# Split operands for the value products and memory scores of a hybrid decoder layer, with other warm-up products and other places for the turns of x

## Time and profile before

| | us |
|---|---|
| median of 3 runs | 573.56 (573.34 to 574.38) |
| profiled execution | 572.92 |
| its span, first to last instruction | 571.1 |
| TensorE busy | 562.1 (98%) |
| VectorE busy | 425.9 (75%) |
| ScalarE busy | 406.6 (71%) |

### The profile page before, as it was taken

How to read it: one execution, slowest core, us unless ns; L and a number is a source line. 1 busy time by engine, 2 the same in 40 slices (tenths; PEclk the granted TensorE clock), 3 DMA queues, 4 the chain that set the end, 5 groups by cost and what they waited for, 6 DMA issues and landing times.

```text
span 571.1 us, 8602 instructions
## 1 busy us (share of the span) xinstructions
PE 562.1 (98%) x2640; PEld 468.0 (82%) x2640; DVE 425.9 (75%) x716; ACT 406.6 (71%) x651; POOL 2.1 (0%) x26
## 2 busy tenths in 40 slices
PE   8999999999999999999999999999999999999994
PEld 7888888888888888888888888888888888888884
DVE  4769769678886877866756768668568886877975
ACT  5786866967868778776784784875598786855543
POOL 1000000000000000000000000000000000000000
PEclk9999999999999999999999999999999999999998
DMA  8997769568676776886875976779799986983803
GB/s 272 353 280 238 210 173 250 169 201 230 190 233 192 200 216 188 234 224 163 250 215 157 264 199 192 220 194 299 246 229 266 260 248 187 260 230 111 244 2 147
DMA packets 151236, 123.32 MB, mean 216 GB/s; under 512 B 66809, under 2 KB 133162, under 8 KB 150698
## 3 DMA queue, kind: packets, MB, share of 16 engines
q1 hardware_dynamic: 151112, 122.98, 76.3%
q10 hardware_dynamic: 98, 0.03, 0.0%
HBM read 105.93 MB, written 2.10 MB: 189 GB/s over the span
## 4 chain that ended last, share of the span: by engine, by line
PE 98%; DVE 1%; ACT 0%; POOL 0%; issue 0%; ACTq 0%; POOLq 0%
PE ps L614 28%; PE ps L615 28%; PE ps L616 28%; PE ps L697 2%; PE ps L650 1%; PE ps L654 1%; PE ps L658 1%; PE ps L679 1%; PE ps L850 1%; PE ps L855 1%; PE ps L851 1%; PE ps L637 1%; PE ps L772 1%; PE ps L624 0%; PE ps L818 0%; PE ps L682 0%
## 5 line engine op out<-in xcount | busy, mean ns | idle before, releaser
L1209 DVE TENSOR_TENSOR w_lo<-w_raw,w_hi 128x1024 fp32r<-128x1024 f32 x183 | 222.5, 1222 | 106.2 <-ACT w_hi L880 104.2
L880 ACT ACTIVATE w_hi<-w_raw 128x1024 fp32r<-128x1024 f32 x183 | 192.6, 1057 | 82.3 <-PE ps L616 81.3
L614 PE MATMUL ps<-w_hi,aT 128*128 128x512 f32 x540 | 211.8, 392 | 0.0
L615 PE MATMUL ps<-w_lo,aT 128*128 128x512 f32 x540 | 210.3, 389 | 0.0
L616 PE MATMUL ps<-w_hi,aT 128*128 128x512 f32 x540 | 210.1, 389 | 0.0
L616 PEld LDWEIGHTS ps<-w_hi,aT 128*128 128x128 f32 x540 | 101.4, 188 | 21.2
L614 PEld LDWEIGHTS ps<-w_hi,aT 128*128 128x128 f32 x540 | 101.4, 188 | 21.0
L615 PEld LDWEIGHTS ps<-w_lo,aT 128*128 128x128 f32 x540 | 101.4, 188 | 20.4
L614 PE MATMUL ps<-w_hi,yT_hi 128*128 128x512 f32 x144 | 56.2, 390 | 0.0
L616 PE MATMUL ps<-w_hi,yT_lo 128*128 128x512 f32 x144 | 56.0, 389 | 0.0
L615 PE MATMUL ps<-w_lo,yT_hi 128*128 128x512 f32 x144 | 56.0, 389 | 0.0
(11 more groups left out here) (202 smaller groups left out, 569.1 us busy)
## 6 DMA issues: line engine op xcount, KB each, us to landing
w_raw<-in_w_in SPq DMA_DIRECT2D x251, 256.0 KB, 3.2
w_raw<-in_w_out SPq DMA_DIRECT2D x64, 256.0 KB, 4.0
w_raw<-in_w_kv_mem SPq DMA_DIRECT2D x32, 256.0 KB, 4.5
w_raw<-in_w_q_mem SPq DMA_DIRECT2D x16, 256.0 KB, 3.0
w_raw<-in_w_o_mem SPq DMA_DIRECT2D x16, 256.0 KB, 3.8
mems<-in_mem SPq DMA_DIRECT2D x1, 2048.0 KB, 10.1
xs<-in_x SPq DMA_DIRECT2D x3, 512.0 KB, 6.3
w_raw<-in_w_in SPq DMA_DIRECT2D x10, 128.0 KB, 5.5
```

What stands on the lines that cost most here:

```text
L614: pe.matmul(acc, hi[:, k0 + k, tok], w_hi[:, slot, k], start=first and k == 0, stop=False)
L615: pe.matmul(acc, hi[:, k0 + k, tok], w_lo[:, slot, k], start=False, stop=False)
L880: act.activation(w_hi[:, i % SPLITS], raw, ACT.Copy).then_inc(hi_made, 1)
L1209: dve.tensor_tensor(lo, w_raw[:, i % RAW], hi.bitcast(F32), ALU.subtract).then_inc(lo_made, 1)
```

## The change

- Value products: `v_sb` becomes `v_hi` (ScalarE, same instruction) and `v_lo` (VectorE, at n = 3 and 4); `probT` gets a high copy (ScalarE, behind the merge at n = 4) and a low difference (VectorE, n = 5). Each of the three products of a head becomes three fp32r products. VectorE's `silu_piece` stands at n = 4, 6, 7, 8. `probT_hi`, `probT_lo` and `v_lo` live in tiles that were free then.
- Memory scores: both banks of turned queries and the turned keys are split into high parts (ScalarE) and low parts (VectorE), and each of the 8 products becomes three fp32r products.
- Warm-up: 10 and 6 products instead of 3 and 2, of a 128x128 tile of ones that VectorE sets; TensorE waits for that tile and no longer for the identity in front of them.
- x turns: row blocks 2 and 3 inside k-tile 1, 4 and 5 inside k-tile 3, both ahead of the tile's last pair of products. The three gain vectors are loaded from SP's queue behind half 2 and turned behind k-tile 6.
- Lambda: the product that spreads it has 128 rows: the tile of ones, and a column that is zero except in its first element.

```diff
-ROWS_BEHIND = {0: (2,), 1: (3,), 2: (4, 5), 4: (6, 7), 6: (8, 9, 10, 11), 10: (12, 13, 14, 15)}
+ROWS_AMID = {1: (2, 3), 3: (4, 5)}
+ROWS_BEHIND = {4: (6, 7), 6: (8, 9, 10, 11), 10: (12, 13, 14, 15)}
-WARM_UP = (3, 2)
+WARM_UP = (10, 6)
+SILU_AT = (4, 6, 7, 8)
...
 # SP, load of the first halves
+                if n == 2:
+                    for row, vec in ((0, norm_mem_g), (KO, mem_norm_g)):
+                        sp.dma_start(gains[row:row + KO, :], ...).then_inc(gains_loaded, 16)
+                    sp.dma_start(gains[2 * KO:2 * KO + 1, :], subln_g).then_inc(gains_loaded, 16)
 # TensorE
-                    pe.matmul(ps[:, 2, 0:P], ident[:, :], ident[:, :], start=True, stop=True)
+                    pe.matmul(ps[:, 2, 0:P], ones, ones, start=True, stop=True)
...
+                    for later in ROWS_AMID.get(k, ()):
+                        transpose_rows(later)
                     pe.wait_ge(k_lo if i == 0 and n < SINGLE else lo_made, n + 1)
                     for t in range(NT):
                         m = pe.matmul(ps[:, t, :], aT_hi[:, k, t * P:(t + 1) * P], w_lo[:, slot, i],
...
-                    if k == 1:
+                    if k == 6:
                         transpose_gains()
...
-                            m = pe.matmul(ps[:, 4 + u, t * P:(t + 1) * P], probT[:, u, i], v_sb[:, kt, head],
-                                          start=kt == 0, stop=kt == t)
+                            acc = ps[:, 4 + u, t * P:(t + 1) * P]
+                            pe.matmul(acc, probT_hi[:, u, i], v_hi[:, kt, head], start=kt == 0, stop=False)
+                            pe.matmul(acc, probT_hi[:, u, i], v_lo[kt][:, head], start=False, stop=False)
+                            m = pe.matmul(acc, probT_lo[:, u, i], v_hi[:, kt, head], start=False, stop=kt == t)
...
-                            pe.matmul(ps[:, 6, SEQ:SEQ + 1], ones_row[:, :], neg_lam_row[0:1, :], ...)
+                            pe.matmul(ps[:, 6, SEQ:SEQ + 1], ones, neg_lam_row[:, :], ...)
...
+            pe.wait_ge(ones_ready, 1)
+            keep_busy(WARM_UP[0])
             pe.wait_ge(ident_ready, 2)
-            keep_busy(WARM_UP[0])
...
-                        m = pe.matmul(ps[:, (4, 0)[t] + h // 2, ...], qmT_sb[:, h, ...], kmT_sb[:, h, :], ...)
+                        pe.matmul(acc, qmT_hi[:, h, tok], kmT_hi[:, h], start=True, stop=False)
+                        pe.matmul(acc, qmT_hi[:, h, tok], kmT_lo[:, h], start=False, stop=False)
+                        m = pe.matmul(acc, qmT_lo[h // 2][:, h % 2, tok], kmT_hi[:, h], start=False, stop=True)
 # ScalarE
+                    act.activation(probT_hi[:, u], probT[:, u], ACT.Copy).then_inc(probT_hi_ready, 1)
...
+                    act.activation(kmT_hi[:, :, :], kmT_sb[:, :, :], ACT.Copy).then_inc(kmT_hi_ready, 1)
...
+                    for b in range(2):
+                        act.activation(qmT_hi[:, 2 * b:2 * b + 2], ps[:, 4 + b, :]..., ACT.Copy)
 # VectorE
-                if n in (4, 5, 6, 7):
-                    silu_piece(a, n - 4)
+                if n in (3, 4):
+                    dve.scalar_tensor_tensor(v_lo[t], ps[:, 2 + t, 0:2 * P], r_x[:, t:t + 1],
+                                             v_hi[:, t].bitcast(F32), ALU.mult, ALU.subtract)
+                if n == 5:
+                    for u in range(2):
+                        dve.tensor_tensor(probT_lo[:, u], probT[:, u], probT_hi[:, u].bitcast(F32), ALU.subtract)
+                if n in SILU_AT:
+                    silu_piece(a, SILU_AT.index(n))
...
+            dve.memset(ones, 1.0).then_inc(ones_ready, 1)
...
+                    dve.tensor_tensor(kmT_lo[:, :, :], kmT_sb[:, :, :], kmT_hi[:, :, :].bitcast(F32), ALU.subtract)
...
+                    for b in range(2):
+                        dve.tensor_tensor(qmT_lo[b][:, :, :], ps[:, 4 + b, :]..., qmT_hi[:, 2 * b:2 * b + 2]..., ALU.subtract)
```

More of the change, by code:

```diff
@@ L199, in program @@
         r_rows = y_sb[:, :, 0:P]
+        ones = r_row[:, 0:P]
         junk_row, _ = carve(pool, 0, DM)
@@ L206, in program @@
         vm_sb = qm_sb
-        qmT_sb, at = carve(pool, at, 4, SEQ)
+        _, at = carve(pool, at, 4, SEQ)
         kmT_sb, at = carve(pool, at, 4, SEQ)
@@ L326, in program @@
         ones_ready = sem("ones_ready")
+        lam_zeroed = sem("lam_zeroed")
         lam_made = sem("lam_made")
@@ L342, in program @@
         gate_ready = sem("gate_ready")
-        v_ready = sem("v_ready")
+        v_hi_ready = sem("v_hi_ready")
+        v_lo_ready = sem("v_lo_ready")
         silu_steps = sem("silu_steps")
@@ L355, in program @@
         probT_ready = sem("probT_ready")
+        probT_hi_ready = sem("probT_hi_ready")
+        probT_lo_ready = sem("probT_lo_ready")
         pv_made = sem("pv_made")
@@ L370, in program @@
         qmT_made = sem("qmT_made")
-        qmT_ready = sem("qmT_ready")
+        qmT_hi_ready = sem("qmT_hi_ready")
+        qmT_lo_ready = sem("qmT_lo_ready")
+        kmT_hi_ready = sem("kmT_hi_ready")
+        kmT_lo_ready = sem("kmT_lo_ready")
         km_ready = sem("km_ready")
@@ L410, in program @@
         kT_rows = kT_parts[:, :, :, :].rearrange("p u r s -> p (u r) s")
+        probT_hi = cT_hi[:, 0:3].rearrange("p a s -> p (a s)").rearrange("p (u i q) -> p u i q", u=2, i=3)
+        probT_lo = cT_lo[:, 0:3].rearrange("p a s -> p (a s)").rearrange("p (u i q) -> p u i q", u=2, i=3)
+        v_lo = (cT_hi[:, 3], cT_lo[:, 3])
+        qmT_hi = kT_rows
+        qmT_lo = (qT_hi, qT_lo)
+        kmT_hi, kmT_lo = cT_hi, cT_lo
         def qm_rows(g, hf):
@@ L509, in _ @@
                     load_pair_half(DIFF, 0, 0, n)
+                if n == 2:
+                    for row, vec in ((0, norm_mem_g), (KO, mem_norm_g)):
+                        sp.dma_start(gains[row:row + KO, :], vec[0].rearrange("(k p) -> k p", p=P)
+                                     ).then_inc(gains_loaded, 16)
+                    sp.dma_start(gains[2 * KO:2 * KO + 1, :], subln_g).then_inc(gains_loaded, 16)
                 if n == 6:
@@ L588, in _ @@
                                   2.0 ** (-8.0 * (h + 1) / HEADS)).then_inc(consts_ready, 1)
-            pool_e.memset(ones_row[:, :], 1.0).then_inc(ones_ready, 1)
         @block.tensor
@@ L716, in pair_window @@
                             pe.wait_ge(gainsT_ready, 3)
-                        wait(pe, v_ready, 2 * j)
+                        wait(pe, v_lo_ready, 2 * j)
                     if first and n < PAIR_HALVES // 2:
@@ L728, in pair_window @@
                             m.then_inc(r_row_made, 1)
-                            pe.wait_ge(ones_ready, 1)
                             pe.wait_ge(lam_ready, 2)
-                            pe.matmul(ps[:, 6, SEQ:SEQ + 1], ones_row[:, :], neg_lam_row[0:1, :], start=True, stop=True
+                            pe.matmul(ps[:, 6, SEQ:SEQ + 1], ones, neg_lam_row[:, :], start=True, stop=True
                                       ).then_inc(lam_made, 1)
@@ L766, in memory_scores @@
             def memory_scores():
-                pe.wait_ge(qmT_ready, 2)
-                pe.wait_ge(kmT_ready, 2)
+                pe.wait_ge(qmT_lo_ready, 2)
+                pe.wait_ge(kmT_lo_ready, 1)
                 for t in range(NT):
                     for h in range(4):
-                        m = pe.matmul(ps[:, (4, 0)[t] + h // 2, (h % 2) * SEQ:(h % 2 + 1) * SEQ],
-                                      qmT_sb[:, h, t * P:(t + 1) * P], kmT_sb[:, h, :], start=True, stop=True)
+                        acc = ps[:, (4, 0)[t] + h // 2, (h % 2) * SEQ:(h % 2 + 1) * SEQ]
+                        tok = slice(t * P, (t + 1) * P)
+                        pe.matmul(acc, qmT_hi[:, h, tok], kmT_hi[:, h], start=True, stop=False)
+                        pe.matmul(acc, qmT_hi[:, h, tok], kmT_lo[:, h], start=False, stop=False)
+                        m = pe.matmul(acc, qmT_lo[h // 2][:, h % 2, tok], kmT_hi[:, h], start=False, stop=True)
                     m.then_inc(scores_m_made, 1)
@@ L780, in _ @@
                 if (what, n, g) == ("out", 1, 0):
-                    pe.wait_ge(v_ready, 2 * PAIRS)
+                    pe.wait_ge(v_lo_ready, 2 * PAIRS)
                 if (what, n, g) == ("out", 2, 0):
@@ L937, in chunk_b_out @@
                 act.activation(gate_sb[:, t], gate, ACT.Identity, scale=r_x[:, t:t + 1]).then_inc(gate_ready, 1)
-                act.activation(v_sb[:, t], ps[:, 2 + t, 0:2 * P], ACT.Identity, scale=r_x[:, t:t + 1]
-                               ).then_inc(v_ready, 1)
+                act.activation(v_hi[:, t], ps[:, 2 + t, 0:2 * P], ACT.Identity, scale=r_x[:, t:t + 1]
+                               ).then_inc(v_hi_ready, 1)
             def merge_probabilities(a):
@@ L1064, in _ @@
             act.activation(warm, warm, ACT.Exp).then_inc(warm_ready, 1)
-            for row, vec in ((0, norm_mem_g), (KO, mem_norm_g)):
-                act.dma_start(gains[row:row + KO, :], vec[0].rearrange("(k p) -> k p", p=P)).then_inc(gains_loaded, 16)
```

(37 more changed lines are left out.)

8 lines of the change are left out of this document (4 added, 4 removed).

## The result

The changed kernel takes 580.65 us (median of 4 runs, 580.44 to 580.86) against 573.45: ratio 1.012, 95% interval 1.0105 to 1.0135. Its profiled execution took 580.86 us with a span of 579.1, 8.0 us more than that of before. Executions of over 800 us (two of the run with scores and lambda alone, one of the run with the early tile of ones) are disturbed ones and count in no ratio.

The account below looks back on a forecast made before the run. TensorE was taken as the bound, busy 562.1 of 571.1 us. Value products +5.9, memory scores -0.6 and head +2.7 sum to +8.0: 580.9 us, or 581.6 on the scale of the medians, range 575.8 to 583.8.

Parts of the forecast that it names:

- both ranges: Whole kernel's time: 575.8 to 583.8 us overall, and the main forecast's own range of 579.5 to 583.5.
- Value products: Value block of each head pair: 18 products at 0.112 us take 2.07 against 1.34, +5.9 us for 8 pairs.
- Memory scores: Memory scores: 24 products of 256 columns take 2.83 us against 3.45, -0.6, with the extra copies costing nothing.
- New splits: Copies and differences on ScalarE and VectorE in each pair: hidden, 2.8 us spare, so no cost.
- Head: Kernel start: later first product +2.4, given back -1.0, stalls at x turns +1.3, in all +2.7 us.
- The 1.0 given back: Head: slow first pair, stall at the x turns and slow first pair of tile 2 vanish, -1.0 us.
- the stated range of the head: Head in all: from +0.5 to +3.5 us around the forecast +2.7.
- Lambda: Product that spreads lambda: 128 rows instead of one, same one column and same load columns, so 0.
- the 8.0 forecast: Sum for the whole kernel: 5.9 - 0.6 + 2.7 = +8.0 us on the profiled execution.

Follow-up runs that it names:

- the run with the early tile of ones: Kernel before plus split memory scores, lambda's 128-row product, and 3 and 2 warm-up products of the tile of ones: median 572.99 us, ratio 0.9994.
- the first experiment: Changed kernel with only the value products put back to float32, without their new splits, SiLU pieces at old places: 575.01 us.

## Why the prediction was right

Forecast 581.6, measured 580.65, inside both ranges. By its own steps:

- *Value products*, +0.73 per pair at a slot of 0.112: the slot is 0.112, the block 2.01 instead of 2.07, +5.4. The reading behind it, that the load of the stationary operand sets the slot of a short product, was only argued there; the two runs with halved operands bear it out. The undone edit gives 5.6.
- *Memory scores*, -0.6: -0.58, and the copies in front of them are hidden.
- *New splits*, nothing: VectorE's differences of the probabilities end at 75.0 and the block begins at 77.97, 3 us spare, as forecast (2.8). The last pair shows no wait either.
- *Head*, +2.7: +3.1. Gain turn 5.79 (forecast 5.55), first real product 8.11 (8.0), rise of the clock near 6.4 (6.3), stalls 0.73 each (0.65). The 1.0 given back was too much: the 0.67 pair that followed the gains turn moved with it to tile 7. The stall had the right cause, but 1.39 us from the start of the turns instead of 1.55, and a slow pair behind it (0.70 for 0.46) that the sum didn't have. The match in the rise is luck: the three runs that kept this head's instructions rose near 4.3, 5.8 and 6.5. And the stated range of the head, +0.5 to +3.5, doesn't follow from its own bounds, which give +0.7 (1.7 - 1.0 + 0) and +3.7 (3.2 - 1.0 + 1.5).
- *Lambda*, 0: this step was wrong, -0.28. I counted columns only. In the timeline of before the one-row product starts 0.31 us after the first of the two turns ahead of it, in the changed kernel 0.22, and the wide one behind takes 0.43 against 0.34. The cause isn't separated: the rows changed from 1 to 128 and its operands with them. The semaphore waits aren't it: the run with scores and lambda alone has the same two ahead of the product, and its product is quick.
- The median moved by 7.2, the profiled executions by 8.0: the profiled one of before lay below its median, that of after above. That the 8.0 forecast is also the 8.0 of the profiled executions is partly luck: the block came 0.5 under its term and lambda 0.3, the head 0.4 and the windows 0.3 over theirs.

The forecast's sum hides one error of understanding. I treated the ten warm-up products as pure delay with a given rise of the clock. The run with three of them contradicts it: its median shows no gain, and in its trace the rise came near 9.0. What the number of products does to the rise stays open, since traces of the same head differ by 2 us.

## What to carry to other kernels

Three fp32r products replace one float32 product with a gain only where the moving operand has enough columns to hide the load of the stationary one. At the two sizes measured here, with 128 stationary columns, they lose at 128 moving columns (0.34 against 0.22 us) and win at 256 (0.36 against 0.43). Look for the floor in the product *behind* a short one, or in the spacing of the weight loads. A turn whose result passes through another engine wants a whole tile of products behind it, as it had before. Warm-up products that run past the landing of the first data delay the real ones: the long head with the turns put back takes 579.5, the old head 577.89 (they differ in the warm-up's tile and the gain loads too). How many pay isn't shown: with the turns inside the tiles ten are no worse than three, and five show no gain clear of the noise.

## What the runs showed that I had not expected

The moment at which the clock rises differs between executions of the same head. A warm-up record starts every 0.21 us at the lower level and every 0.11 at the higher; by these rows, and in the shorter heads by the first real products, the level rose near 6.4 in the changed kernel and near 5.8, 4.3 and 6.5 in the three runs with the same head instructions, and over all traces between 4.3 and 9.0 us, with first products at 1.1 to 1.7. One trace can't tell what a warm-up does to it.

It is also not what sets the end of the old head. In the kernel before and the three runs that have its turns and three and two warm-up products the rise came near 6.4, 5.2, 5.6 and 6.8, but the first 8 halves end at 31.97, 32.03, 31.74 and 31.98: all four wait for x ahead of the turn of row block 2.

The long warm-up makes the time steady: 19 executions of before on one chip lie between 572.45 and 575.14, the ten of the first experiment, with the ten warm-up products, on that chip between 574.97 and 575.32. From the end of the first 8 halves to the end of the span, the changed kernel and the three runs that differ from it in the head alone take 543.98 to 544.01 us, so it is most likely in the head that executions differ. Whether it is the landing of x and of the first weights, which ten products cover, or the clock isn't shown: of the other executions there is no trace.

The product of a one-row tile by one column took 0.28 us more, with the one behind it, than the one with 128 rows; why stays open.
